# A mixture-of-experts stage with its flips on VectorE, its weight rows laid out anew, and four gate units shared by all chunks

## The reference

```python
logits = h @ router_w + router_b
top_v, top_i = lax.top_k(logits, 4);  gates = softmax(top_v)
# for every expert e, for the tokens sent to it:
gu   = x @ w_gate_up[e] + b_gate_up[e]        # 1024 -> 2048
gate = min(gu[:1024], 7); up = clip(gu[1024:], -7, 7)
act  = (up + 1) * gate * sigmoid(1.702 * gate)
y    = act @ w_down[e] + b_down[e]            # 1024 -> 1024
out[token] += gates[token, e] * y
```

## Time and profile before

| | us |
|---|---|
| median of 3 runs (lowest, highest) | 1429.55 (1427.65, 1431.92) |
| the profiled execution | 1427.33 |
| its span, first to last instruction | 1425.6 |
| PE busy | 1286.2 |
| DVE busy | 496.2 |
| ACT busy | 324.7 |
| jobs loop, from the first bias product to the last down product | 316.3 to 1386.4 |

### The profile page before, as it was taken

How to read it: one execution, slowest core, us unless ns; L and a number is a source line. 1 busy time by engine, 2 the same in 40 slices (tenths; PEclk the granted TensorE clock), 3 DMA queues, 4 the chain that set the end, 5 groups by cost and what they waited for, 6 DMA issues and landing times.

```text
span 1425.6 us, 33985 instructions
## 1 busy us (share of the span) xinstructions
PE 1286.2 (90%) x12484; PEld 560.1 (39%) x12485; DVE 496.2 (35%) x1476; ACT 324.7 (23%) x649; POOL 299.4 (21%) x348
## 2 busy tenths in 40 slices
PE   6999999959998999999999999888999899988870
PEld 3764544543333434444444333333443333433320
DVE  2002222443334333333333344342334333343337
ACT  2023332221312222222222222221223222222211
POOL 0513332011212212222212112130212212111210
PEclk9999999969999999999999999999999999999995
DMA  9512110224999999999989999998999989999967
GB/s 379 208 59 74 60 74 1 104 83 173 415 386 415 394 413 395 368 365 366 366 366 365 392 418 416 417 416 352 366 367 417 413 362 414 393 417 416 417 248 294
DMA packets 90869, 454.86 MB, mean 319 GB/s; under 512 B 14049, under 2 KB 14489, under 8 KB 55774
## 3 DMA queue, kind: packets, MB, share of 16 engines
q1 hardware_dynamic: 77902, 430.86, 74.5%
q0 software_dynamic: 12512, 22.11, 4.3%
q10 hardware_dynamic: 432, 1.57, 0.3%
HBM read 444.23 MB, written 14.71 MB: 322 GB/s over the span
## 4 chain that ended last, share of the span: by engine, by line
PE 73%; DMA 21%; DVE 3%; issue 1%; ACT 1%; POOL 0%; SPq 0%; DVEq 0%; POOLq 0%
PE bank L661 35%; DMA arena<-in_w_gate_up 20%; PE bank L687 14%; PE bank L421 7%; PE bank L491 4%; PE bank L437 3%; PE bank L648 2%; PE bank L626 2%; PE bank L706 1%; PE bank L450 1%; DVE xs L1284 1%; PE bank L478 1%; PE bank L464 1%; PE bank L707 1%; PE bank L616 1%
## 5 line engine op out<-in xcount | busy, mean ns | idle before, releaser
L661 PE MATMUL bank<-arena,hT 128*32 128x512 f32 x5120 | 583.9, 606 | 30.2 <-DMA arena<-in_w_gate_up 27.9
L687 PE MATMUL bank<-arena,hT 128*32 128x256 f32 x5120 | 308.4, 386 | 33.1 <-ACT hT L859 33.1
L661 PEld LDWEIGHTS bank<-arena,hT 128*32 128x32 f32 x5120 | 157.3, 111 | 393.0 <-issue 341.1
L1241 DVE TENSOR_TENSOR arena<-bank,gain 128x512 f32<-128x512 f32 x128 | 88.4, 691 | 402.0 <-PE bank L661 402.0
L687 PEld LDWEIGHTS bank<-arena,hT 128*32 128x32 f32 x5120 | 159.6, 111 | 161.3 <-issue 77.3
L963 POOL DMA_DIRECT2D ahead<-in_consts x98 | 51.6, 530 | 641.1 <-DVE hT L1260 615.3
L876 ACT ACTIVATE arena<-arena 128x256 f32<-128x256 f32 x128 | 53.3, 417 | 560.1 <-DVE arena L1243 558.7
L1260 DVE TENSOR_TENSOR hT<-bank,gain 128x256 f32<-128x256 f32 x128 | 51.4, 422 | 212.2 <-PE bank L687 206.1
L980 POOL DMA_INDIRECT y_rows<-hT,arena x80 | 82.4, 1029 | 158.3 <-DVE hT L1260 150.7
L421 PE MATMUL bank<-hT,arena 128*128 128x512 f32 x224 | 103.6, 610 | 0.8 <-ACT hT L764 0.8
L966 POOL DMA_INDIRECT hT<-h_rows,arena x82 | 84.8, 1035 | 67.9 <-issue 34.0
(11 more groups left out here) (146 smaller groups left out, 857.9 us busy)
## 6 DMA issues: line engine op xcount, KB each, us to landing
arena<-in_w_gate_up SPq DMA_DIRECT2D x256, 1024.0 KB, 6.6
arena<-in_w_down SPq DMA_DIRECT2D x128, 1024.0 KB, 15.3
arena<-in_w_in SPq DMA_DIRECT2D x10, 1024.0 KB, 18.1
arena<-y_rows SPq DMA_DIRECT2D x8, 1024.0 KB, 12.3
arena<-in_w_out SPq DMA_DIRECT2D x4, 1024.0 KB, 22.0
arena<-bias_by_dist POOLq DMA_DIRECT2D x6, 512.0 KB, 4.0
xs<-in_x SPq DMA_DIRECT2D x4, 512.0 KB, 7.4
h_rows<-arena POOLq DMA_DIRECT2D x4, 512.0 KB, 2.9
```

The lines of the kernel that those rows point to most:

```text
L661: mm = pe.matmul(bank[c][j * CH:(j + 1) * CH, :].rearrange("p (g n) -> p g n", g=2), xT[:, c, (k % 2) * P + (k // 2) * CH:(k % 2) * P + (k ...
L687: mm = pe.matmul(bank[c][j * CH:(j + 1) * CH, 0:Q], aT[:, c, (k % 2) * P + (k // 2) * CH:(k % 2) * P + (k // 2 + 1) * CH], w[:, j * Q:(j + ...
L1241: dve.tensor_tensor(gu[:, b, :], bank[c][:, :], bt[:, 0:2 * Q], ALU.add).then_inc(gu_read, 1)
```

## The change

- **Weight rows.** Because VectorE flips only inside blocks of 32 x 32, the contraction index is dealt otherwise: partition 32j+i of a unit now holds row 256j + 32u + i of `w_gate_up`, so a unit is four pieces of 32 rows, 2 MB apart. A unit of `w_down` gives partition 32j+i the two neighbouring rows 256j + 64u + 2i and the next, 8 KB in one run; its four pieces are 1 MB apart. The destination, one ring slot of 128 partitions, is as it was.
- **Flips.** `dve.transpose` turns x (`flip_x`) and the activation; PE's flips, the PSUM banks for them and ACT's copies are gone.
- **Biases.** ACT's queue loads four rows of 3 KB for each job onto partitions 0, 32, 64 and 96; `stream_shuffle` on DVE spreads them. The table `bias_all` and the products with `pick` are gone.
- **Gate units 0 to 3** are each used for all chunks of the job in one go, then each chunk does units 4 to 7 by itself.
- **Chunk counts.** Every engine branches on the job's number of chunks (at least 2). DVE and ACT skip chunks that are absent, and POOL's tiny DMAs go. One semaphore counts all gathers, one all scatters; thresholds come from a table of running sums, which has two rows more.

```diff
             def load_unit(e, u):
                 if u < KT:
-                    src = w_gate_up[bass.ds(e, 1), u * P:(u + 1) * P, :].rearrange("e p n -> p (e n)")
-                    dst = ring[:, u, :]
+                    src = w_gate_up[bass.ds(e, 1)].rearrange("e (j k i) n -> (e k) j i n", j=4, i=CH)[u]
                 else:
-                    a = (u - KT) * 2 * P
-                    src = w_down[bass.ds(e, 1), a:a + 2 * P, :].rearrange("e (k p) n -> p (e k) n", p=P)
-                    dst = ring[:, u, :].rearrange("p (k n) -> p k n", k=2)
+                    src = w_down[bass.ds(e, 1)].rearrange("e (j u i k) n -> (e u) j i (k n)", j=4, k=2, i=CH)[u - KT]
+                dst = ring[:, u, :]
                 sp.dma_start(dst, src).then_inc(unit_full[u], 16)
...
+                def gate_step(c, k):
+                    w = ring[:, k, :].rearrange("p (g n) -> p g n", g=2)
+                    for j in range(4):
+                        mm = pe.matmul(bank[c][j * CH:(j + 1) * CH, :].rearrange("p (g n) -> p g n", g=2),
+                                       xT[:, c, k * CH:(k + 1) * CH], w[:, :, j * Q:(j + 1) * Q],
+                                       start=(k == 0), stop=(k == KT - 1), tile_position=(0, j * CH))
+                    if k == KT - 1:
+                        mm.then_inc(gu_done, 1)
+                    elif c == 0:
+                        mm.then_inc(units_used, 1)
+
+                def gates_together(chunk_list):
+                    for k in range(KT // 2):
+                        pe.wait_ge(unit_full[k], job * 16 + 16)
+                        for c in chunk_list:
+                            if k == 0:
+                                pe.wait_ge(y_done, before_job + (AHEAD - 1 if c else AHEAD))
+                            gate_step(c, k)
+
+                def gate_rest(c):
+                    for k in range(KT // 2, KT):
...
-                pe.wait_ge(pick_done, job + 1)
-                pe.matmul(bank[4][:, 0:2 * Q], pick, bias_all[:, 0:2 * Q], start=True, stop=True).then_inc(bias_mm, 1)
-                pe.matmul(bank[5][:, 0:Q], pick, bias_all[:, 2 * Q:3 * Q], start=True, stop=True).then_inc(bias_mm, 1)
-                pe.wait_ge(x_copied, job * 2 + 2)
                 indices(job + 1)
+                pe.wait_ge(x_done, job + 1)
                 with pe.If(chunks > 2):
                     with pe.If(chunks > 3):
-                        gate(3, every)
-                        gate(2, every, flip=3)
...
+                        gates_together((2, 1, 0))
+                    gate_rest(2)
+                with pe.Else():
+                    gates_together((1, 0))
+                gate_rest(1)
+                gate_rest(0)
...
+            def load_bias(e):
+                act.dma_start(bias_row[0:P:CH, :], biases[bass.ds(e * 4, 4), :])\
+                    .then_inc(bias_in, 16)
...
+            def flip_x(c, last):
+                ins = dve.transpose(xT[:, c, :], xg[:, c, :])
...
+                    dve.tensor_tensor(act_q[b], up, sg[:, b, :], ALU.mult).then_inc(actq_done, 1)
+                    dve.wait_ge(actq_done, low + (AHEAD - c))
+                    dve.transpose(aT[:, c, :], act_q[b].rearrange("p (u i k) -> p u k i", k=2, i=CH)).then_inc(act_done, 1)
...
+                dve.wait_ge(y_done, before_job + AHEAD)
+                dve.wait_ge(bias_in, job * 16 + 16)
+                dve.sem_inc(waited_dve, 1)
+                dve.stream_shuffle(bt, bias_row[:, :], [0] * CH).then_inc(bias_spread, 1)
```

More of the change, by code:

```diff
@@ L65 @@
 FREED = JOB_UNITS - 2
-ORDER = tuple(range(NCH))[::-1]
+LEAST = 2
+AHEAD = NCH - 1
 JOBS_MAX = 49
+COUNT_MAX = 2 + NCH * JOBS_MAX
 FAR = 4096
@@ L81 @@
 C_FIRST = 472
-C_END = 473
+C_AFTER = 473
+C_END = C_AFTER + 49
+ROWS = 5
 def bucket_of(dist):
@@ L618, in indices @@
                 mm.then_inc(idx_mm, 1)
[L620 to L628, removed]
             indices(0)
             pe.wait_ge(jdiag_done, 1)
-            pe.matmul(bank[1][:, 0:3 * JOBS_MAX], ones, jdiag, start=True, stop=True).then_inc(jobs_mm, 1)
@@ L633, in _, with run_job @@
-            pe.wait_ge(idx_done, 1)
-            flip_x(0, 0)
-            flip_x(0, 1)
+            pe.matmul(bank[1][:, 0:ROWS * JOBS_MAX], ones, jdiag, start=True, stop=True).then_inc(jobs_mm, 1)
             pe.wait_ge(jobs_done, 2)
[L638 to L656, removed]
+            def run_job(job, chunks, before_job, low):
+                def gate_step(c, k):
[17 more added lines that the diff above has]
+                    for k in range(KT // 2, KT):
@@ L681, in down @@
+                def down(c, ks):
+                    pe.wait_ge(act_done, low + (AHEAD - c))
                     for k in ks:
@@ L725, in run_job @@
                         down(3, every)
[L726 to L733, removed]
+                    down(2, every)
+                down(1, every)
                 down(0, every)
@@ L876, in _ @@
                     act.activation(sg[:, c % 2, :], gu[:, c % 2, 0:Q], ACT.Sigmoid, scale=ALPHA)\
                         .then_inc(sig_done, 1)
-                    if n >= 1:
-                        copy_act(job, n - 1)
-                copy_act(job, NCH - 1)
-                copy_x(job + 1, 0)
-                copy_x(job + 1, 1)
-            act.wait_ge(dn_done, all_down)
+                act.wait_ge(bias_spread, job + 1)
+                load_bias(e)
+                with act.If(chunks > 2):
+                    with act.If(chunks > 3):
+                        sigmoid(3)
+                    sigmoid(2)
@@ L903, in link @@
                 pool.wait_ge(pstep, steps[0])
-            for c in range(NCH):
-                pool.dma_start(ahead[0:16, 1, c, :], consts[0:16, 4 * c:4 * c + 4])\
-                    .then_inc(scattered[c], 16)
+            for a in range(2):
+                pool.dma_start(ahead[0:16, a, :], consts[0:16, 4 * a:4 * a + 4]).then_inc(scattered, 16)
+            pool.memset(bias_row[:, :], 0.0).then_inc(bias_zero, 1)
             link(pool.memset(pb[:, :, 0:8], 0.0))
@@ L996, in _, with scatter @@
+                def scatter(c):
+                    pool.wait_ge(y_done, low + (AHEAD - c))
+                    pool.sem_inc(waited_pool, 1)
+                    pool.indirect_dma_start(y_rows, bass.IndirectOffsetOnAxis(ap=idx_s[:, c:c + 1], axis=0),
+                                            yb[:, c, :], None, bounds_check=last_row, oob_is_err=False)\
+                        .then_inc(scattered, 16)
                 pool.wait_ge(idx_done, job + 2)
-                pool.wait_ge(x_tr, job * 2 + 2)
+                pool.wait_ge(x_done, job + 1)
@@ L998, in _ @@
                 pool.sem_inc(waited_pool, 1)
-                gather(next_chunks)
-                for n, c in enumerate(ORDER):
-                    pool.wait_ge(y_done, job * NCH + (NCH + n + 2))
-                    pool.sem_inc(waited_pool, 1)
-                    if c == 0:
-                        scatter_chunk(c)
-                        continue
-                    with pool.If(chunks > c):
-                        scatter_chunk(c)
-                    with pool.If(chunks <= c):
-                        signal(c, scattered[c], 1)
@@ L1010, in _ @@
-            for c in range(NCH):
-                pool.wait_ge(gathered[c], njobs * 16 + 16)
+                with pool.If(next_chunks > 2):
+                    with pool.If(next_chunks > 3):
+                        gather(3, gathered)
+                    gather(2, gathered)
+                gather(1, gathered)
+                gather(0, gathered)
+                with pool.If(chunks > 2):
+                    with pool.If(chunks > 3):
+                        scatter(3)
+                    scatter(2)
@@ L1217, in _ @@
                 .then_inc(gate_in, 1)
+            def flip_x(c, last):
+                ins = dve.transpose(xT[:, c, :], xg[:, c, :])
+                if last:
+                    ins.then_inc(x_done, 1)
+            dve.wait_ge(gathered_first, 16 * NCH)
+            for c in range(NCH):
+                flip_x(c, c == NCH - 1)
             job_columns(1, None, link)
-            job_picker(0)
             link(dve.tensor_copy(keep_s, idx_t[:, :, 1]))
@@ L1247, in _ @@
-                    dve.wait_ge(t_done, job * NCH + max(n, 1))
-                    dve.wait_ge(sig_done, job * NCH + (n + 1))
-                    dve.tensor_tensor(act_q[b], up, sg[:, b, :], ALU.mult).then_inc(act_done, 1)
-                job_picker(e)
+                    dve.tensor_scalar(up, up, LIMIT, -LIMIT, ALU.min, ALU.max).then_inc(up_clamped, 1)
+                    dve.wait_ge(gate_clamped, low + (AHEAD - c))
+                    dve.wait_ge(up_clamped, low + (AHEAD - c))
+                    dve.scalar_tensor_tensor(up, up, 1.0, gate, ALU.add, ALU.mult).then_inc(prod_done, 1)
@@ new lines, in _ @@
+                dve.wait_ge(y_done, before_job + AHEAD)
+                dve.wait_ge(bias_in, job * 16 + 16)
+                dve.sem_inc(waited_dve, 1)
```

(33 more changed lines are left out.)

183 lines of the change are left out of this document (82 added, 101 removed).

## The result

The changed kernel takes 4107.4 us (median of 4 runs, 4105.0 to 4110.4) against 1428.6 for the kernel before in the same runs: a ratio of 2.880, with a 95% interval of 2.873 to 2.887. The forecast was 4150, the range 4000 to 4450.

The account below looks back on a forecast made before the run. Before, PE bound three-chunk jobs and loads two-chunk ones; after, loads on four engines bound every job. Loads ending at 4103, plus 5 for last products and 39 for the end, gave 4147, with 1.7 outside 4149, forecast 4150; range 4000 to 4450.

Parts of the forecast that it names:

- The step that decided: Weight loads: 20 missing signals on SP's queue mean outermost rows are dealt equally to up to 16 engines that divide them.
- The choice between 4 and 16: Weight loads: source's four pieces against slot's 128 rows; four engines at about today's rate had 0.75, sixteen with the gain 0.14.
- The price: Weight loads on four engines: 395 MB at 104.5 GB/s, 3780 us, 10.1 us a unit.
- The end: After the loop, from the last down product to the kernel's end: 39 us, as before.
- the last products: PE's work after the last weight unit arrives: 4 to 9 us, depending on its clock level.
- A job: In the loop, each job lasts 122 us, whether it has two or three chunks.
- The first rival: Weight loads: the slot's 128 rows decide, all sixteen engines work, loop 998 instead of 1070, about 1360 us; chance 0.14.
- the chain was to be nearly all DMA into `arena`: Sign of four engines in the profile after: the chain would be nearly all DMA into `arena`.
- the several tens of us that were said: Sign for gate units: median time from issue to landing would rise from 6.6 us to several tens.

Follow-up runs that it names:

- pieces4: The kernel before with only the source of the weight loads changed, to four pieces of 32 rows, 2 MB apart (1 MB for `w_down`): 4118.7 us.
- pitch: The changed kernel with partition p of unit u holding row 8p + u, so 128 outermost rows on both sides: 1364.1 us, ratio 0.958.
- perm: The changed kernel with the weight loads of before and the columns permuted at the norm's output and in the products: 1379.0 us, ratio 0.968.
- split4: The changed kernel with each unit's load cut into four DMAs, one for each piece of 32 rows and its 32 partitions: median 1609.6 us.
- bshare: The kernel before with only the shared use of gate units 0 to 3 added: 1712.8 us, ratio 1.202.

## Why the prediction was right

- *The step that decided* was the count of signals on the small loads. It said that rows are dealt out in equal shares, and left open which side decides; I took the source's 4. pieces4 and the packet count show it: one edit, 4119 us. The choice between 4 and 16 was an argument with no row behind it, and had a chance beside it.
- *The price*: 104.5 GB/s on four engines was 1.4% low. The first of these loads was issued at 328.2 (timeline above), not at 321, since PE began its first gate product at 322.4; the last unit let PE go on at 4060.0, not 4103. With the same 2 us of latency that is 395.3 MB in 3730 us, 106.0 GB/s. The end was 39 us as said, from 4067.4 to 4106.1, and the last products took 7.4 us, in the 4 to 9 given. So 4107 against 4150 is 50 us of a rate mis-sized by 1.4%, with about 10 us back from the late start and the last products.

```profile
322.41 22.80 PE L634 MATMUL bank<-arena,hT 128*32 128x512 f32 x184 [3.33 <-issue]
...
4060.03 7.35 PE L667 MATMUL bank<-arena,hT 128*32 128x256 f32 x80 [7.91 <-DMA arena<-in_w_down]
```

- *A job*: 121.1 us from one job's start on SyncE to the next, 119.8 for the one after; 122 was said.

```profile
1025.23 0.44 SPq L368
...
1146.28 0.45 SPq L368
...
1266.03 0.44 SPq L368
```

- *The first rival* was near as a sum: with sixteen engines the rest of the change is worth 1358 by the prediction, and pitch has 1364. That close a fit is in part luck: the sum had 415 GB/s, which is perm's rate, and perm has 1379, where pitch moves 420. A three-chunk job in pitch takes PE 33.3 us (32.3 said), 20.81 + 10.36 of products and 2.1 between:

```profile
538.35 20.81 PE bank L634 x192
559.16 10.36 PE bank L667 x192
571.67 20.81 PE bank L634 x192
```

- *Missed*: the chain was to be nearly all DMA into `arena`; it is SyncE held in its issues (83%), the same cause under another name. The page after gives no landing time for a unit, so the several tens of us that were said can't be compared. And I said that sixteen engines give 1358 however they are reached. They don't: with sixteen pieces, or with four DMAs, the engines are all busy and slow (2004, 1610).

## What to carry to other kernels

Before reshaping a load, look at the outermost count of its source and of its destination. In these runs the weights came at the full rate only where both counts were 128 in one DMA. If a layout needs pieces, look for a permutation with one stride (row 8p + u here) in place of blocks. A busy share of the DMA engines tells how many work, GB/s tells how well; look at both. And a gain on the compute side, here 3 us a job, is worth nothing until the load beneath it has been priced for its shape.

## What the runs showed of the hardware that was not expected

- Sixteen busy engines moved 238 GB/s when a load was cut into sixteen pieces of eight rows and partitions, and 232 or 233 when a DMA filled 32 or 64 partitions from neighbouring rows, against 414 to 420 when one DMA filled all 128 row by row. Distance between source rows wasn't the cause (245 with near pieces, 417 from 400 to 1300 us with rows 64 KB apart). The exception is split4, 346 with 32 partitions and far rows, and it is unexplained.
- Four or eight engines at work keep about 26 GB/s each (109 at a share of 0.26, 214 at 0.52), also with pieces 1 to 2 MB apart; all sixteen have 25 to 26 each.
- VectorE's flip of x, 128 x 256, took 411 ns from a dense source and 610 from every eighth column (pitch); in neither kernel did it bound a job.
- SyncE's issue of a DMA lasted 9.1 to 9.6 us in most rows of the loop after, about a load's time, where the kernel before had 0.33 us at the median.
- Some unrolled products more in PE's loop went with 20% more time, and with 153 packets of instructions in place of 15 (bshare).

```profile
L1169 DVE STREAM_TRANSPOSE hT<-hT 128x256 f32<-128x256 f32 x83 | 46.8, 610 | 0.0
```
